# Linear attention with 32-row tiles and three level batches a chunk, LRU input projections between them, gate projections behind

## The chip, the cores and the metric

The kernel runs on one core of a Trainium2 chip. The metric is the device time of one execution in microseconds; lower is better. TensorE (PE) multiplies, with its weight loads (PEld) as records of their own; VectorE (DVE), ScalarE (ACT) and GpSimd (POOL) work elementwise; SyncE (SP) starts transfers.

## What is computed

Two layers of a hybrid decoder over 1024 tokens of width 1024, all in float32. Each layer normalises its input to h, projects it with one matrix, runs four mixers beside each other, gates and projects back:

```python
h = rms_norm(x, norm_g)
(gate, a_q, a_k, a_v, a_g, b_q, b_k, b_v, b_f, c_q, c_kv, c_kr, d_x) = jnp.split(h @ w_in, points, axis=-1)
ya = gla_mixer(a_q, a_k, a_v, a_g, ...)      # gated linear attention, 8 heads, 32 key and 64 value columns each
yb = fox_mixer(...)                          # softmax attention with a forget gate
yc = mla_mixer(...)                          # latent attention
yd = rglru_mixer(d_x, ...)                   # convolution of width 4, two gates, linear scan
y = jnp.concatenate([ya, yb, yc, yd], axis=-1) * jax.nn.silu(gate)
return x + y @ w_out
```

The linear attention (group A) is a scan over chunks of positions. Inside a chunk, with G the cumulated log decay of each key column:

```python
A = jnp.sum(q_[:, :, :, None, :] * k_[:, :, None, :, :] * decay, axis=-1)    # decay = exp(G_t - G_s), s <= t
o = einsum('bhtk,bhkv->bhtv', q_ * exp(G), S) + einsum('bhts,bhsv->bhtv', A, v_)
S_new = exp(G_last)[..., None] * S + einsum('bhsk,bhsv->bhkv', k_ * exp(G_last - G), v_)
```

and its output is normalised per head. Group D (the LRU) is `h = a * h_before + b` over positions, with a and b from two gates.

## The kernel before

**Projections.** h lies in SBUF as two tiles, `h_hi` (rounded) and `h_lo` (the rest), both 128 partitions (8 blocks of the contraction) by 1024 tokens. w_in comes in chunks of mostly 256 columns (1 MB each) into two sets of buffers used in turn. `load_chunk` (SP) waits until the last chunk of its set is split; `round_chunk` (ScalarE, L186) makes `w_hi`, when the last unit of the set's earlier chunk is done; `split_chunk` (GpSimd, L193) makes `w_lo`. `project` computes a unit of output in one PSUM bank with 24 matmuls, 8 for each of the products w_hi h_hi, w_hi h_lo, w_lo h_hi (L227). A chunk of kind "C" has 4 units of 512 columns, one of kind "T" 8 units of 256. Units take banks 0 to 3 in turn (`RING = 4`), and `wait_bank` makes TensorE wait until the unit four before has been taken out. The names: q, k and v1, v2 (group A), gA0, gA1 and gD0, gD1 (gates), dx0, dx1 (LRU input), fq1, fk1, fv1 (group B), outA, outD (parts of the output projection, L478, added to the rows by VectorE at L508).

**Order.** Each engine runs one in-order program, written out by hand (`tensor_gla`, `scalar_lru`, `vector_gla`, `gpsimd_program`, `sync_gla` and so on), with semaphores between them. TensorE does q, `turn_a`, k, `z`, gA0, gA1, then eight chunks of linear attention, gD0 and outA; then the LRU stage: dx0, gate products of channel block 0 (`gates_pe`, L981, 4 matmuls), two units of gD1, block 1, gD1, dx1, block 2, fq1 with block 3 in it, fk1, fv1, outD.

**Linear attention** (`Gla`). q and k are held transposed: two groups g of 128 partitions, each with 4 heads of 32 partitions. A chunk has 128 tokens. Its causal matrix A is split by 7 levels: at level j blocks of 64 >> (j-1) tokens are paired, and the scores of the later half against the earlier half are a product of decayed queries and keys with exponents taken relative to the edge between them, so that all are below zero. The diagonal comes from one undecayed product. So a chunk has 9 items (`NI`): 2 diagonal ones and 7 levels.
- `exponent` (VectorE, L702 and L703, 14 passes of 128x128) writes G relative to the edges to E; `decay` (ScalarE, L812 to L815) exponentiates it.
- `expand_q` (ScalarE, L805, 4 passes) writes q4, four copies of q, in which a head mask leaves one head each. Thus one matmul with 128 rows of contraction gives the scores of four heads side by side.
- `chunk_pool` (GpSimd) makes decayed keys `kl` (L680, 7 passes of 128x256) and the expanded decayed queries `ql` of levels 2, 4, 6; `expand` (L666, two passes a level) on VectorE makes the others. Both have three slots.
- `products_pe` (TensorE) computes an item into one of four banks: a diagonal item is one matmul of 512 columns (L853), a level two of 256 (L864).
- `mask` (VectorE) puts an item into A: the diagonal by a product with the identity (L715, 128x512), a level by a predicated copy (L724, 128x512).
- `finish` (TensorE), a chunk later and behind the first five items of the next: transposes of the end keys (L876), the output product (L882 with the state S, L885 with A, 8 matmuls of 64 columns), the state product (L892).
- Then `state` (VectorE, L756, 8 pieces of 32x64), squares, `means`, root, `normalise` (L768), and `turn_y` and `y_evac`, which transpose a chunk of output and multiply it by its gate.

A float32 matmul shows as two records of load and two of matmul, an fp32r one as one of each.

**Products with 64 output partitions.** In the softmax attentions `pv` (L1379) writes 64 output partitions, for the even head 0 to 63, for the odd one 64 to 127; two calls follow each other. L1318 and L367 are transposes, as L902.

**LRU** (`Lru`). For each of four blocks of 128 channels: `conv` (VectorE, L1007, L1009), `gates_pe`, `gates_act` (ScalarE sigmoids, L1022, L1025), `gx`, `decay_act` (Tanh L1037, Exp L1040, Square L1043), `u`, `root_act` (Sqrt L1055), `scan` (VectorE, L1061 to L1065). ScalarE loads a table (ACT_TABLE_LOAD) between kinds of functions. `zero_blocks` (GpSimd) and `load_blocks` (SP) prepare the gate weights. `sync_fox` loads outD's rows and weights when the last scan is done.

Of the kernel before, what the change touches and what calls it, by code (L numbers as in the profile page):

```python
# [24 lines left out]
HH = 4  # L25
# [18 lines left out]
RING = 4  # L44
# [40 lines left out]
class Trunk:  # L85


    def __init__(self, nc, dram, out, ctx):
# [23 lines left out]
        self.chunks, self.chunk_of, self.units, self.unit_of = [], {}, [], {}  # L112
        self.w_landed = [self.sem(f"w_landed{i}") for i in range(2)]
# [31 lines left out]
    def add_unit(self, layer, name, part, by):  # L145
        j = self.chunk_of.get((layer, name))
        if j is not None:
            self.chunks[j]["units"].append(len(self.units))
        nth = 1 + sum(1 for unit in self.units if unit[2] == by)
        self.unit_of[layer, name, part] = len(self.units)  # L150
        self.units.append((j, part, by, nth))
# [49 lines left out]
    def bank(self, u):  # L201
        return self.psum[:, u % RING, :]

    def wait_bank(self, pe, u):
        if u >= RING:
            _, _, by, nth = self.units[u - RING]
            pe.wait_ge(self.evac_sem[by], nth)

    def project(self, pe, layer, name, *part):
        u = self.u(layer, name, *part)  # L210
        j, part, _, _ = self.units[u]
# [3 lines left out]
        self.wait_bank(pe, u)  # L215
        if first:
            pe.wait_ge(self.w_rounded, j + 1)
        for n, (w, h) in enumerate(((w_hi, self.h_hi), (w_hi, self.h_lo), (w_lo, self.h_hi))):
            if n == 2 and first:
                pe.wait_ge(self.w_split, j + 1)  # L220
            for kk in range(KT):
                if c["kind"] == "C":
                    m, half = part
                    lhs, rhs, o = w[:, kk, m * P:(m + 1) * P], h[:, kk, half * BANK:(half + 1) * BANK], self.bank(u)
                else:
                    lhs, rhs, o = h[:, kk, part * P:(part + 1) * P], w[:, kk, :], self.bank(u)[:, :width]
                last = pe.matmul(o, lhs, rhs, start=(kk == 0 and n == 0), stop=(kk == KT - 1 and n == 2))  # L227
        last.then_inc(self.unit_done, 1)
# [10 lines left out]
    def evacuated(self, eng, layer, name, *part):  # L239

        _, _, by, nth = self.units[self.u(layer, name, *part)]
# [20 lines left out]
def plan_layer(k, layer):  # L262
# [24 lines left out]
    chunk("k", "C", C_AK, CHUNK, 1)  # L287
    gate("gA0", 0, 0, 0)
# [3 lines left out]
    chunk("dx0", "C", C_DX, CHUNK, 1)  # L292
    gate("gD1", 3, 1, 0)
    chunk("dx1", "C", C_DX + CHUNK, CHUNK, 1)
# [216 lines left out]
class Gla:  # L511


    NI = GN + LEVELS
    MIDDLE = GN + 3
    HALF = P // 2
    IN, END = LEVELS, LEVELS + 1
    NB, B_OUT, B_STATE, B_KT, B_Y = 4, 4, 5, 6, 7
    ON_POOL = (2, 4, 6)
    ON_DVE = (1, 3, 5, 7)  # L520
    R = 3
    N16 = SEQ // BANK

    def __init__(self, k, layer):
        self.k, self.layer = k, layer
        HALF, NI = self.HALF, self.NI
        self.qT = k.area("gla_qT", A_QT, [P, GN, SEQ])
        self.kT = k.area("gla_kT", A_KT, [P, GN, SEQ])
        self.v = k.area("gla_v", A_V, [P, TT, GROUP_W])
        self.G = k.area("gla_G", A_GATE0, [P, GN, SEQ])  # L530
        self.sg = k.area("gla_gate", A_SG, [P, CT, SEQ])
        self.E = k.area("gla_E", A_E, [P, 2, LEVELS + 2, GN, P])
        self.aT = k.area("gla_aT", A_E, [RANK, SEQ])
        self.e = k.area("gla_e", A_E + 4096, [P, GN, SEQ])
        self.k_et = k.area("gla_k_end_tok", 84032, [P, GN * P])
# [8 lines left out]
        self.rstd = k.area("gla_rstd", s + 1280, [P, HEADS])  # L544
        self.a_tok = k.area("gla_a", A_TOK, [P, TT, RANK])
        w = W_SET[1]
        self.S = k.at("gla_S", w, [P, GN, HH, HEAD])
        self.masks = k.at("gla_masks", w + 2048, [P, LEVELS, HALF], I32)
        self.q4 = k.at("gla_q4", w + 3840, [P, GN, HH, P])
        w += SET  # L550
        self.A = k.at("gla_A", w, [P, 2, HEADS, P])
        self.ql = k.at("gla_ql", w + 8192, [P, self.R, GN, HH, HALF])
        self.kl = k.at("gla_kl", w + 14336, [P, self.R, GN, P])
        n = {"gla_loaded": 80, "masks_loaded": 16, "a_turned": self.N16, "a_copied": self.N16, "z_done": GN * self.N16,
             "z_biased": GN * self.N16, "logs": 1, "exponents": TT, "decays": TT, "q_expanded": TT,
# [2232 lines left out]
```

## Time and profile before

| what | value |
|---|---|
| time, median of 3 runs | 2696.1 us (2695.87 to 2705.18) |
| profiled execution, from first to last instruction | 2699.1 us |
| TensorE busy | 2458.8 us, 91% |
| VectorE, ScalarE, GpSimd busy | 1280.1, 972.9, 862.0 us |
| share of TensorE in the chain that ended last | 79% |
| linear attention chunks, layer 1 | 172.4 to 355.3 us |
| linear attention chunks, layer 2 | 1510.5 to 1693.3 us |

The span is that of one profiled execution, and no other time of that execution is shown. Busy time counts a record from its start to its end; matmul records overlap, so a busy TensorE can still have room. The chain follows the last instruction back to what released it, step by step.

### The profile page before, as it was taken

The page shows a single profiled execution, that of the slowest core. Times are in us where ns is not written, and L with a number is a line of the kernel's source. Part 1 is how long each engine was busy: PE and PEld are TensorE (multiplying, and loading weights), DVE is VectorE, ACT ScalarE, POOL GpSimd, SP SyncE. Part 2 cuts the span into 40 slices and gives each one's busy share as a digit, 9 for nine tenths or more (in the row PEclk, how much of TensorE's full clock was granted, in tenths as well). Part 3 has the DMA queues.
Part 4 walks back from the last instruction along what each step waited for, and adds up shares of the span by engine and source line. Part 5 has one row for each costly group of instructions (what it writes and reads, how often), then busy time and mean ns, then how long its engine had stood idle before and what let it go on. Part 6 is the DMA issues. An engine that isn't in the chain of part 4 may idle for free.

```text
span 2699.1 us, 32797 instructions
## 1 busy us (share of the span) xinstructions
PE 2458.8 (91%) x13104; PEld 1870.4 (69%) x13104; DVE 1280.1 (47%) x1966; ACT 972.9 (36%) x1596; POOL 862.0 (32%) x726
## 2 busy tenths in 40 slices
PE   7977699998999999899999766999989999998998
PEld 7755477897577695655697555779865866856556
DVE  4049934543514325565431698236344153265653
ACT  4232214632433433344433222155324243333441
POOL 1225522211441620154411455121205225202542
PEclk9988899999999999999999888999999999999999
DMA  4100043041010021200321000422300101122003
GB/s 137 51 0 1 1 132 107 17 156 47 1 48 1 13 74 57 95 23 1 126 79 35 1 1 1 160 79 69 135 16 1 48 1 45 42 89 85 1 1 117
DMA packets 91864, 141.15 MB, mean 52 GB/s; under 512 B 18208, under 2 KB 65344, under 8 KB 91712
## 3 DMA queue, kind: packets, MB, share of 16 engines
q1 hardware_dynamic: 91712, 139.05, 15.1%
q8 instruction: 105, 1.72, 0.3%
q14 instruction: 47, 0.39, 0.0%
HBM read 105.48 MB, written 33.55 MB: 52 GB/s over the span
## 4 chain that ended last, share of the span: by engine, by line
PE 79%; DVE 15%; issue 3%; ACT 2%; POOL 1%; DMA 0%; POOLq 0%; SPq 0%; DVEq 0%; ACTq 0%
PE psum L227 36%; PE psum L478 12%; PE psum L1379 6%; PE psum L1364 4%; PE psum L1333 3%; PE psum L1365 3%; PE psum L1367 3%; PE psum L864 3%; PE psum L1346 2%; PE psum L1318 2%; DVE gla_E L703 2%; DVE gla_ql L666 2%; DVE gla_A L724 2%; PE psum L1386 1%; DVE gla_S L756 1%
## 5 line engine op out<-in xcount | busy, mean ns | idle before, releaser
L193 POOL TENSOR_TENSOR w_lo<-w_raw,w_hi 128x2048 fp32r<-128x2048 f32 (+3 forms) x60 | 278.2, 4638 | 970.5 <-ACT w_hi L186 970.5
L864 PE MATMUL psum<-gla_ql,gla_kl 128*128 128x256 f32 x448 | 147.5, 484 | 115.4 <-DVE gla_ql L666 111.7
L864 PEld LDWEIGHTS psum<-gla_ql,gla_kl 128*128 128x128 f32 x448 | 105.8, 248 | 162.1 <-DVE gla_A L724 112.4
L227 PE MATMUL psum<-h_hi,w_hi 128*128 128x512 f32 x768 | 199.3, 403 | 0.0
L1577 POOL TENSOR_TENSOR mla_acc<-mla_acc,mla_p 128x512 f32<-128x512 f32 (+3 forms) x160 | 160.2, 1015 | 107.9 <-ACT mla_p L1447 106.5
L227 PE MATMUL psum<-w_hi,h_hi 128*128 128x256 f32 (+3 forms) x1280 | 186.2, 289 | 4.7 <-ACT w_hi L186 4.7
L227 PE MATMUL psum<-h_lo,w_hi 128*128 128x512 f32 x768 | 190.1, 390 | 0.0
L227 PE MATMUL psum<-h_hi,w_lo 128*128 128x512 f32 x768 | 189.8, 390 | 0.0
L227 PE MATMUL psum<-w_hi,h_lo 128*128 128x256 f32 (+3 forms) x1280 | 182.2, 286 | 0.0
L227 PE MATMUL psum<-w_lo,h_hi 128*128 128x256 f32 (+3 forms) x1280 | 179.8, 283 | 1.8 <-POOL w_lo L193 1.8
L186 ACT ACTIVATE w_hi<-w_raw 128x2048 fp32r<-128x2048 f32 (+3 forms) x60 | 113.4, 1894 | 187.1 <-PE psum L478 174.3
L1577 POOL TENSOR_TENSOR fox_acc<-fox_acc,fox_p 128x512 f32<-128x512 f32 (+3 forms) x160 | 148.7, 946 | 89.6 <-ACT fox_p L1447 88.8
L227 PEld LDWEIGHTS psum<-w_hi,h_hi 128*128 128x128 f32 x1280 | 167.4, 194 | 10.9 <-issue 9.3
L508 DVE TENSOR_TENSOR x_rows<-x_rows,psum 128x512 f32<-128x512 f32 x128 | 85.7, 685 | 180.1 <-PE psum L478 152.1
L227 PEld LDWEIGHTS psum<-h_hi,w_hi 128*128 128x128 f32 x768 | 146.3, 193 | 34.5 <-issue 4.9
L227 PEld LDWEIGHTS psum<-w_hi,h_lo 128*128 128x128 f32 x1280 | 167.8, 195 | 0.0
L227 PEld LDWEIGHTS psum<-w_lo,h_hi 128*128 128x128 f32 x1280 | 164.9, 192 | 2.2 <-POOL w_lo L193 2.2
L227 PEld LDWEIGHTS psum<-h_lo,w_hi 128*128 128x128 f32 x768 | 144.7, 188 | 30.4
L227 PEld LDWEIGHTS psum<-h_hi,w_lo 128*128 128x128 f32 x768 | 144.2, 188 | 29.9
L680 POOL TENSOR_TENSOR gla_kl<-gla_kT,gla_E 128x256 f32<-128x256 f32 x112 | 90.4, 815 | 214.7 <-PE psum L864 113.8
L1447 ACT ACTIVATE fox_p<-psum 128x512 f32<-128x512 f32 (+1 forms) x192 | 94.0, 489 | 136.6 <-PE psum L1369 109.1
L1447 ACT ACTIVATE mla_p<-psum 128x512 f32<-128x512 f32 (+1 forms) x192 | 93.8, 489 | 132.8 <-PE psum L1369 106.3
(321 smaller groups left out, 4827.7 us busy)
## 6 DMA issues: line engine op xcount, KB each, us to landing
w_raw<-in_w_in_dram SPq DMA_DIRECT2D x38, 1024.0 KB, 5.2
out_dram<-x_rows SPq DMA_DIRECT2D x64, 512.0 KB, 2.7
x_rows<-out_dram SPq DMA_DIRECT2D x56, 512.0 KB, 5.6
w_raw<-in_w_out_dram SPq DMA_DIRECT2D x16, 1024.0 KB, 5.2
x_first<-in_x_dram SPq DMA_DIRECT2D x8, 512.0 KB, 7.4
x_rows<-in_x_dram SPq DMA_DIRECT2D x8, 512.0 KB, 6.6
w_raw<-in_w_in_dram SPq DMA_DIRECT2D x2, 1088.0 KB, 8.9
w_raw<-in_w_in_dram SPq DMA_DIRECT2D x2, 1056.0 KB, 5.1
```

What stands on the lines that cost most here:

```text
L186: act.activation(self.w_hi[c["set"]][:, :n], self.w_raw[c["set"]][:, :n], ACT.Copy).then_inc(self.w_rounded, 1)
L193: pool.tensor_tensor(self.w_lo[c["set"]][:, :n], self.w_raw[c["set"]][:, :n], self.w_hi[c["set"]][:, :n].bitcast(F32), ALU.subtract).then_ ...
L227: last = pe.matmul(o, lhs, rhs, start=(kk == 0 and n == 0), stop=(kk == KT - 1 and n == 2))
L478: last = pe.matmul(k.bank(u), y, w[:, c, :], start=(c == 0 and i == 0), stop=(c == CT - 1 and i == 2))
L508: dve.tensor_tensor(at, at, ps, ALU.add).then_inc(k.evac_sem["dve"], 1)
L680: pool.tensor_tensor(self.kl[:, m % self.R, :, :], self.kT[:, :, self.tok(c)], self.E[:, c % 2, j - 1, :, :], ALU.mult).then_inc(self.k_le ...
L864: last = pe.matmul(k.psum[:, n % self.NB, g * HH * self.HALF:(g + 1) * HH * self.HALF], self.kl[:, m % self.R, g, :], self.ql[:, m % self. ...
L1333: last = pe.matmul(out, q[:M_ROW, a, x * P:(x + 1) * P], kk[:M_ROW, a, :hi - lo], start=True, stop=not diagonal)
L1364: pe.matmul(out, self.k_hi[ks][:R, a, keys], self.q_hi[qs][:R, a, lo:], start=True, stop=False)
L1379: pe.matmul(self.k.psum[a * HEAD:(a + 1) * HEAD, 4 + i % 2, lo:], self.pairs[p]["v"](a, kb), self.p[:, u % self.PR, lo:], start=(kb == 0), ...
L1447: act.activation(self.p[:, u % self.PR, lo:], self.k.psum[:, u % 2, lo:], ACT.Exp).then_inc(self.exp_done.sem, 1)
L1577: pool.tensor_tensor(acc, acc, p, ALU.add).then_inc(self.acc_done.sem, 1)
```

## The change

**Score products.** The queries are no longer expanded. Each head's scores come from a matmul of its own with 32 rows of contraction, the head's 32 partitions (a row tile of TensorE), and go to the bank of the head's number in its group (banks 4 to 7). `level_products` multiplies, in E itself, only the earlier halves by the keys, and writes the later halves times the queries to `ql`, on GpSimd alone: two passes of 128x128 a level. A chunk has three batches: the diagonal with levels 1, 2; levels 3, 4, 5; levels 6, 7. Between batches TensorE runs one of the three products of a dx unit (`product`, a third of `project`), unit c of dx0 and dx1 in chunk c. `mask_batch` masks a batch, the diagonal in one pass of 1024 columns; A has one buffer. The state S is 128 x 2 x 64, its product is 8 matmuls of 32 output columns, and VectorE writes a copy `S_bd` with zeros between heads for the output product.

**Order.** `turn_a` and `z` go between the q units. gA0 and gA1 come behind the chunks; their units have the y transposes between them, now four token tiles of one channel block at a time (`GROUPS` = 8). The dx units use banks 2 and 3 alone (`k.ring`). ScalarE evacuates dx inside the chunks. The first two convolutions run ahead of outA's additions. In the LRU stage the gate products are: blocks 0 and 1 after two units of gD1, block 2 after 7 parts of fq1, block 3 after one part of fk1; ScalarE and VectorE treat blocks in pairs, and ScalarE takes out all fq1 parts ahead of the third block's sigmoids. Several tiles have other places in SBUF.

```diff
     def chunk_pool(self, pool, c):
...
+        for b, levels in enumerate(self.BATCHES):
+            if c >= 1:
+                pool.wait_ge(self.scored.sem, self.scored.at(self.NBATCH * (c - 1) + b + 1))
+            for level in levels:
+                last = self.level_products(pool, c, level)
+            last.then_inc(self.products.sem, 1)
...
+    def level_products(self, eng, c, level):
+        e = self.halves(self.E[:, c % 2, level - 1, :, :], level)
+        q, kk = (self.halves(x[:, :, self.tok(c)], level) for x in (self.qT, self.kT))
+        eng.tensor_tensor(e[:, :, :, 0, :], kk[:, :, :, 0, :], e[:, :, :, 0, :], ALU.mult)
+        ql = self.ql[:, level - 1, :, :].rearrange("p g (n b) -> p g n b", b=self.HALF >> (level - 1))
+        return eng.tensor_tensor(ql, q[:, :, :, 1, :], e[:, :, :, 1, :], ALU.mult)
...
+    def scores(self, pe, c, b):
+        n = self.NBATCH * c + b
...
+        else:
+            pe.wait_ge(self.masked.sem, self.masked.at(self.OPS * c + self.BATCHES[b][0]))
+        if b == 0:
+            out = self.scores_at(0, -2, P)
+            for g in range(GN):
+                for i in range(HH):
+                    r = slice(DK * i, DK * (i + 1))
+                    pe.matmul(out[:, i, g, :], self.kT[r, g, self.tok(c)], self.qT[r, g, self.tok(c)], start=True, stop=True)
+        pe.wait_ge(self.products.sem, self.products.at(n + 1))
+        for x, level in enumerate(self.BATCHES[b]):
+            out = self.scores_at(b, x, self.HALF)
+            for g in range(GN):
+                for i in range(HH):
+                    r = slice(DK * i, DK * (i + 1))
+                    last = pe.matmul(out[:, i, g, :], self.E[r, c % 2, level - 1, g, :], self.ql[r, level - 1, g, :],
+                                     start=True, stop=True)
+        last.then_inc(self.scored.sem, 1)
...
     def mix_dve(self, dve, link, c):
...
         if c + 1 < TT:
             self.exponent(dve, c + 1)
+        self.mask_batch(dve, c, 0)
         if c >= 1:
+            self.state(dve, link, c - 1)
             self.means(dve, link, c - 1)
+        self.mask_batch(dve, c, 1)
         if c >= 1:
             self.normalise(dve, c - 1)
+        self.mask_batch(dve, c, 2)
...
+    def mix_pe(self, pe, c, between):
+        self.scores(pe, c, 0)
+        if c >= 1:
+            self.finish(pe, c - 1)
+        between(pe, 0)
+        self.scores(pe, c, 1)
+        between(pe, 1)
+        self.scores(pe, c, 2)
+        between(pe, 2)
...
 def tensor_gla(pe, k, a):
...
     for c in range(TT):
-        a.gla.mix_pe(pe, c)
-    a.gla.finish(pe, TT - 1)
+        gla.mix_pe(pe, c, lambda pe, n: k.product(pe, L, f"dx{c // 4}", n, *C_PARTS[c % 4]))
+    k.project(pe, L, "gA0", *C_PARTS[0])
+    gla.finish(pe, TT - 1)
+    k.project(pe, L, "gA0", *C_PARTS[1])
+    pe.wait_ge(gla.normed.sem, gla.normed.at(TT))
+    for i, part in enumerate(C_PARTS[2:]):
+        k.project(pe, L, "gA0", *part)
+        gla.turn_y(pe, i)
+    for i, part in enumerate(C_PARTS):
+        k.project(pe, L, "gA1", *part)
+        gla.turn_y(pe, 2 + i)
...
 def scalar_lru(act, k, link, a):
...
+    for t in range(TT):
+        fox.evac(act, "fq", t)
     lru.gates_act(act, 2)
+    lru.gates_act(act, 3)
     lru.decay_act(act, link, 2)
+    lru.decay_act(act, link, 3)
     lru.root_act(act, 2)
...
     lru.root_act(act, 3)
```

## Rows read from the trace of the kernel before

**Rows 1.** the page's first line
```profile
span 2699.1 us, 32797 instructions
```

**Rows 2.** busy time by stretches: length, then busy us (records) of each engine, granted clock
```profile
172.40:355.30 182.90, 121.02 (x488) 90.19 (x488) 161.70 (x318) 47.79 (x97) 101.60 (x122) 0.82 0.00 1
1510.50:1693.30 182.80, 120.44 (x488) 89.32 (x488) 161.50 (x318) 47.55 (x97) 101.65 (x122) 0.82 0.00 1
...
422.70:571.00 148.30, 148.30 (x898) 129.42 (x897) 76.60 (x56) 88.64 (x113) 29.75 (x6) 1.00 0.21 70
```

**Rows 3.** the chain: start us, us, engine, line, records
```profile
99.00 21.79 PE psum L227 x96
...
510.41 60.63 PE psum L227 x504
...
1345.17 1.75 PE psum L367 x16
```

**Rows 4.** waits from 217 to 342 us: who waits for whom, us, times, longest
```profile
PE psum L864 <- DVE gla_ql L666: 40.6, 16, 5.3
PEld psum L864 <- DVE gla_A L724: 39.9, 11, 5.7
```

**Rows 5.** timeline, L853 and a `finish`: start us, us, engine, line, tiles, records
```profile
243.34 1.88 PE L853 MATMUL psum<-gla_q,gla_kT 128*128 128x512 f32 x4
...
248.92 0.30 PEld L882 LDWEIGHTS psum<-gla_S,gla_E 128*128 128x128 f32 x2
...
250.58 1.08 PEld L885 LDWEIGHTS psum<-gla_v,gla_A 128*128 128x128 f32 x8
...
251.57 0.73 PEld L892 LDWEIGHTS psum<-gla_v,gla_k_end_tok 128*128 128x128 f32 x4
```

**Rows 6.** timeline of TensorE, pairs of `pv`
```profile
698.35 0.44 PE L1379 MATMUL psum<-fox_p,fox_v 128*64 128x128 f32 x4
...
701.14 1.08 PE L1379 MATMUL psum<-fox_p,fox_v 128*64 128x512 f32 x4
```

**Rows 7.** loads of `pv`: ns min/median/max of one; then the timeline of one pair's
```profile
L1379 PEld LDWEIGHTS psum<-fox_p,fox_v x384: 132/135/138, 686.9 to 2269.8; 128*64 128x64 f32 x192
...
701.14 0.20 PEld L1379 LDWEIGHTS psum<-fox_p,fox_v 128*64 128x64 f32 x4 [0.36 <-issue]
```

**Rows 8.** tile gla_A: ns min/median/max of one
```profile
L724 DVE COPY_PREDICATED gla_A<-gla_masks,psum x112: 691/719/1329, 181.9 to 1689.3; 128x512 f32<-128x512 int32 x112
L715 DVE TENSOR_TENSOR gla_A<-psum,ident x32: 672/676/679, 179.4 to 1670.9; 128x512 f32<-128x512 f32 x32
```

**Rows 9.** tile gla_E: ns min/median/max of one
```profile
L703 DVE TENSOR_TENSOR gla_E<-gla_G x112: 275/281/4578, 152.3 to 1654.2; 128x128 f32<-128x128 f32 x112
...
L687 POOL TENSOR_TENSOR gla_E<-gla_qT,gla_E x16: 719/726/767, 188.6 to 1681.7; 128x256 f32<-128x256 f32 x16
```

**Rows 10.** timeline at the first chunk
```profile
175.53 1.68 ACT L812 ACTIVATE gla_E<-gla_E 128x1792 f32<-128x1792 f32 x1
...
178.25 1.86 POOL L680 TENSOR_TENSOR gla_kl<-gla_kT,gla_E 128x256 f32<-128x256 f32 x2 [50.44 <-ACT gla_E L815]
...
189.48 0.81 DVE L702 TENSOR_TENSOR gla_E<-gla_G 128x128 f32<-128x128 f32 x1
```

**Rows 11.** timeline of ScalarE in the LRU
```profile
502.95 0.69 ACT L1022 ACTIVATE lru_dx<-psum,lru_vec 128x512 f32<-128x512 f32 x1
...
508.45 1.28 ACT L1040 ACT_TABLE_LOAD   x1
509.75 1.15 ACT L1040 ACTIVATE lru_dx<-lru_dx,lru_small 128x1024 f32<-128x1024 f32 x1
```

**Rows 12.** timeline of VectorE in the LRU
```profile
496.53 8.16 DVE L1009 SCALAR_TENSOR_TENSOR lru_xc<-lru_dx,lru_conv_w,lru_xc 128x1024 f32<-128x1024 f32 x3
```

**Rows 13.** timeline ahead of outD
```profile
542.64 1.26 SPq L174 DMA_DIRECT2D w_raw<-in_w_out_dram  x2
...
552.51 1.92 ACT L186 ACTIVATE w_hi<-w_raw 128x2048 fp32r<-128x2048 f32 x1 [4.25 <-DMA w_raw<-in_w_out_dram]
```

More of the change, by code:

```diff
@@ L43 @@
 CHUNK_MAX = CHUNK + RANK
-RING = 4
 BASE = 16512
@@ L214, in project @@
         w_hi, w_lo = (w[c["set"]][:, :KT * width].rearrange("p (k n) -> p k n", n=width) for w in (self.w_hi, self.w_lo))
-        self.wait_bank(pe, u)
-        if first:
+        if n == 0:
+            self.wait_bank(pe, u)
+        if n == 0 and first:
             pe.wait_ge(self.w_rounded, j + 1)
[L218 to L228, printed above, removed]
+        if n == 2 and first:
+            pe.wait_ge(self.w_split, j + 1)
+        w, h = ((w_hi, self.h_hi), (w_hi, self.h_lo), (w_lo, self.h_hi))[n]
+        for kk in range(KT):
+            if c["kind"] == "C":
+                m, half = part
+                lhs, rhs, o = w[:, kk, m * P:(m + 1) * P], h[:, kk, half * BANK:(half + 1) * BANK], self.bank(u)
+            else:
+                lhs, rhs, o = h[:, kk, part * P:(part + 1) * P], w[:, kk, :], self.bank(u)[:, :width]
+            last = pe.matmul(o, lhs, rhs, start=(kk == 0 and n == 0), stop=(kk == KT - 1 and n == 2))
+        if n == 2:
+            last.then_inc(self.unit_done, 1)
     def wait_unit(self, eng, layer, name, *part):
@@ L291, in plan_layer @@
     out("outA", 0, 1)
-    chunk("dx0", "C", C_DX, CHUNK, 1)
-    gate("gD1", 3, 1, 0)
-    chunk("dx1", "C", C_DX + CHUNK, CHUNK, 1)
+    gate("gD1", 3, 1, 1)
     chunk("fq1", "T", C_BQ + HALF_W, HALF_W, 0)
@@ L568, in load @@
+         self.out_done, self.state_product, self.state_new, self.squares, self.mean, self.rstd_ready, self.normed,
+         self.y_turned, self.y_ready, self.end_decays) = (Signal(k, name, count) for name, count in n.items())
     def load(self, sp):
@@ L905, in mix_pe @@
[L905 to L908 removed]
+                for i in range(HH):
+                    r = slice(DK * i, DK * (i + 1))
+                    at = GN * P + g * HEAD
+                    last = pe.matmul(k.psum[r, self.B_END, at:at + HEAD], self.k_et[:, g * P + DK * i:g * P + DK * (i + 1)],
+                                     self.v[:, c, g * HALF_W + i * HEAD:g * HALF_W + (i + 1) * HEAD], start=True, stop=True)
@@ L2574, in gpsimd_program @@
             gla.chunk_pool(pool, c)
-            if c == 0:
-                k.split_chunk(pool, L, "gD0")
+            if c == 2:
+                k.split_chunk(pool, L, "dx1")
             if c == 6:
-                a.outA.rest(pool, 0)
-        for name in ("outA0", "outA1", "dx0"):
+                k.split_chunk(pool, L, "gA0")
+        for name in ("gA1", "gD0", "outA0"):
+            k.split_chunk(pool, L, name)
+        for name in ("outA1", "gD1", "fq1"):
             k.split_chunk(pool, L, name)
@@ L2583, in gpsimd_program @@
         a.lru.zero_blocks(pool)
-        for name in ("gD1", "dx1", "fq1", "fk1", "fv1", "outD0", "outD1", "gB1"):
+        for name in ("fk1", "fv1", "outD0", "outD1", "gB1"):
             k.split_chunk(pool, L, name)
@@ L2645, in sync_gla @@
     lru.load(sp)
-    for name in ("outA1", "dx0", "gD1"):
+    for name in ("gD0", "outA0", "outA1", "gD1", "fq1"):
         k.load_chunk(sp, L, name)
@@ L2649, in sync_gla @@
     lru.load_blocks(sp)
-    for name in ("dx1", "fq1", "fk1", "fv1"):
+    for name in ("fk1", "fv1"):
         k.load_chunk(sp, L, name)
```

530 lines of the change are left out of this document (226 added, 304 removed).

## The prediction

> **What bounds the kernel now.** I read the page first: one core, a span of 2699.1 us [rows 1], TensorE busy for 91% of it, and the chain of waits runs over TensorE for 79% of the span. A stage is therefore worth what TensorE idles or wastes in it. The busy time by stretches shows where that is: in the linear attention of either layer (182.9 and 182.8 us) TensorE is busy 121.0 and 120.4 us at a mean granted clock of 0.82, while VectorE is busy for some 162; the projection and LRU stretch behind it runs at 148.3 busy us of 148.3, clock 1.00 [rows 2]. The chain gives the price of a projection: 96 matmuls of 512 columns in 21.79 us, 0.227 each, so a unit of 24 costs 5.45 us; units of 256 columns cost 504 x 0.120, 2.9 us for 24 [rows 3]. The wait table of six chunks names the loop: level matmuls wait for VectorE's expansion (L666) and their loads for its masks (L724) [rows 4]. These are six chunks in 125 us, 20.8 each.
>
> So the linear attention is a ping-pong of VectorE and TensorE with TensorE half empty, and the change can win by filling it. It moves both dx chunks, 8 units, 43.6 us a layer, into the eight row chunks. The stage and these units cost 182.9 + 43.6 = 226.5 us a layer before. All other projections keep their price wherever they stand.
>
> **The decisive unknown: the small matmuls.** Per row chunk the change makes 64 matmuls with 32 rows of contraction (8 of 128 columns, 56 of 64) in place of 2 of 512 and 14 of 256. No row tile is in this trace. The nearest rows are of two kinds. Full-height matmuls of 64 columns (L885): 8 records in 1.08 us, two records to a matmul, 0.27 us each [rows 5]; 64 of them would be 17.3 us a chunk. And column tiles: `pv` (L1379) sends pairs to output partitions 0 to 63 and 64 to 127. A pair takes 1.08 us at 512 columns and 0.44 at 128 [rows 6], where two full-height float32 matmuls of 512 columns (L853) take 1.88 [rows 5]: the pair costs little more than one. Its four loads lie within 0.20 us although each takes 0.135 [rows 7]. So two tiles compute and load at the same time. Four row tiles, each with its own bank (head i of a group goes to bank 4+i), are the same pattern turned. I take four matmuls in the time of one, 0.27 us a round: 16 rounds, 4.3 us a chunk. The bounds are 4.3 below and 17.3 above. I stand near the first, since L1379 is a tile row and L885 is not.
> The Trainium skill ("TensorE: Matmul & The Clock Gate", part 3 on packing small matmuls) states a 3.07-fold gain for four row tiles; by it the 17.3 us would be an estimated 5.6 us and the time some 21 us later than mine; the trace shows the column kind only.
> Each change of tile shape may wait until the array is empty. A pair of 128 columns takes 0.44 us, of which the slope between 128 and 512 columns, 0.64 / 3, explains 0.21 [rows 6]; the other 0.23 is filling and emptying. 8 changes a chunk, 16 chunks: between nothing and 29 us in all. I take 9, nearer to nothing, since filling and emptying lie partly beside the neighbours' and half of the changes fall where TensorE has spare time. "TensorEngine Tiling (Array Packing)" of the Trainium skill (Key Properties) says that a mode switch drains; no row here shows it.
>
> **One chunk, step by step** (us from the start of `scores` batch 0). Batches of 24, 24 and 16 small matmuls cost 1.5, 1.5 and 1.0, and 0.2 until another engine sees them.
> - TensorE: batch 0 until 1.5; `finish` of the chunk before: transposes 0.4, then output product 2.65 (248.92 to 251.57 [rows 5]), seen at 4.7. State product until 5.2 (it was 4 records, now 8 matmuls with 32 output columns; between 0.3 and 1.0, taken 0.6). Then a third of a dx unit, 1.8, until 7.0.
> - VectorE: batch 0 mask from 4.8: one 1024-wide pass 1.3 (two of L715's 0.68) and two of L724 at 0.72 to 0.75 [rows 8], until 7.6. TensorE's batch 1 waits for that: 7.7 to 9.2; dx until 11.0.
> - VectorE: state 1.1 (one pass of 512 columns at 0.68, two small ones) and means 0.95 (the same and a small one) until 9.6; mask batch 1, three times 0.75, until 11.8; normalise 0.7 until 12.5. TensorE's batch 2: 11.9 to 12.9, dx until 14.7. Mask batch 2: 13.1 to 14.5.
> - The next batch 0 starts at 14.7. `exponent`, 14 passes of 0.28 (L703 [rows 9]), runs from 14.5 to 18.4, under the next batch 0 and `finish` (19.5).
> Thus the period is 14.7, with TensorE busy some 13.5 of it. ScalarE (decay 2.8, copies, square, dx evacuation, root: under 6) and GpSimd (14 products of half the width of L687's 0.73 [rows 9], taken 0.45, and two whole: 7.8) are below it. The expansion on VectorE, ScalarE's four q4 copies and the 32-partition state pieces are removed: they are already missing in this sum.
> What queues behind new waits: TensorE's in-order stream puts dx products behind each mask wait, so a late mask delays both. Batch b of `chunk_pool` waits for the same batch a chunk earlier; `decay` ends near 6, so its products have 7 us to spare.
>
> **Beginning and end.** Projections of the output gates used to cover the decay sums and the first exponentials; the k units (21.8 us) cover the sums now, z being moved ahead of them. Not covered: evacuation of the last k part 0.8, table load 1.28 [rows 11], the E passes and a small copy (175.53 to 178.25), together 4.9, and four products 1.8: 7.0 us with scale factors [rows 10]. Chunk 0 has no `finish`: 1.7 + 2.8 + 1.7 + 2.3 + 1.2 + 1.5 = 11.2. Seven more are 102.9. The last `finish` is 3.0, and seven of the eight rounds of y transposes, inside the stage before, now stand beside projections: 4.2. A layer: 7.0 + 11.2 + 102.9 + 3.0 + 4.2 = 128.3 against 226.5, so 98.2 less.
>
> **What is given back.** A split on GpSimd holds a VectorE pass: the longest of L703 took 4.58 us, the length of a split, and ordinary GpSimd products stretch 0.28 to 0.81 [rows 9, 10]. Two splits (dx1, gA0) now fall inside the chunks, as gD0's and outA's did; I charge 4 us a layer.
> The LRU loses the dx units that covered it. With D the end of outA, TensorE runs 2 gD1 units, 4+4 gate products (8 x 0.86), 2 units, 7 fq units: the third gate set is due at D+49, the last fq unit ends at D+55. ScalarE takes all 8 fq parts first and then sigmoids (0.69 each), Tanh, Exp, Square and Sqrt of two channels (1.15 a pass, 1.28 a table load [rows 11]): until D+64 with TensorE's fourth gate set, decays 4.7 and 6.0, roots 3.5, fv1 rounding 1.95: D+80.5. Only then is fk part 0 evacuated. With four banks, fk part 4 waits from D+73 to D+81: 8 us. The block weights' DMA, now behind the fq1 split, comes about 2 us late, the third convolution (up to 8.2 us under a split [rows 12]) 1.5, the bank waits 0.5: 12 us a layer. The scans (about 4.7 each with their two products) end near D+87; outD0's weights take 9.9 us from issue to rounding [rows 13], split near D+108, before TensorE needs them at D+117. Nothing to pay there; 14 us before. DMAs are otherwise moved into idle queues; SP's gD0 load now stands behind `out_done`, 27 us ahead of its use.
>
> **Sum.** 2699.1 - 2 x (98.2 - 4 - 12) + 9 = 2543.7 us of span. The median of the runs shown is 3.0 below that span, so 2541 us. Half a per cent, 13.5 us, is what I count as a difference.
>
> **Rivals.**
> - *Slower chain.* Tiles as taken, but GpSimd's products stretch the masks' neighbours and the period is 17.5 (exponents at L703's 0.81 end after the out product). For it: that row; against it: the exponents have 1.1 us of slack and the masks (L724, median 0.719) seldom stretch. 14 x 2.8 = 39 more: 2580. Chance 0.08.
> - *Half rate.* The two halves of an fp32 matmul go in order, so only two tiles overlap, all that rows 6 show: 8.6 us a chunk, period 19. A layer 15.8 + 133 + 14.2 = 163: 2610. Chance 0.13.
> - *Loads one at a time.* Matmuls overlap, loads of 128 columns don't: two loads of 0.109 (the fastest pace of load and matmul, 16 in 1.75 us in L367 [rows 3]) for each of 64, 14.0 us, period 23.5, 198.7 a layer: 2681. Rows 7 speak against it. Chance 0.12. The same page of the Trainium skill (LDWEIGHTS) says that a 32-row load costs as much as a 128-row load, which is this rival when loads do not overlap.
> - *No overlap, slower than before.* L885's 0.27 for each of the 64: period 27.5, a layer 24 + 192.5 + 14.2 = 230.7, 4 more than before, and the 16 given back stay: 2746. It decides from 0.22 us a small matmul (8 periods of 24). Chance 0.10.
>
> **How the numbers follow.** The forecast has 0.57: 2541, by itself 2500 (no LRU stall, no drains, no split stalls) to 2590. The range goes from 2495 over the slower chain and the half rate to 2670, just short of serial loads. Faster: 0.57 + 0.08 + 0.13 and half of the fourth: 0.84; same 0.07; slower 0.09.
>
> **What would show it.** In the profile after: 24 small matmuls in about 1.5 us (6.5 would be no overlap); dx matmuls between L864's successors; a period near 14.7; clock 1.00 in the chunks; a 7 us gap ahead of the first; a TensorE wait for fk's evacuation of about 8 us. The forecast is wrong if the small matmuls take over 0.1 us each or VectorE's period passes 15.

## The result and the profile after

The changed kernel takes 2560.4 us (median of 4 runs, 2558.3 to 2564.9) beside 2697.3 for the kernel before; the ratio is 0.949 with a 95% interval of 0.947 to 0.950. The forecast was 2541 us with a range of 2495 to 2670. The profiled execution has a span of 2563.1 us, against the 2543.7 that the prediction's sum gives: 19.4 us more. The median is 19.4 us above the forecast too.

Busy time by stretches of the kernel after (start:end, length, then busy us and records of TensorE's matmuls, its loads, VectorE, ScalarE and GpSimd, the granted clock, DMA share, GB/s):

```profile
126.50:261.20 134.70, 112.95 (x1483) 91.86 (x1483) 106.06 (x201) 38.34 (x72) 70.93 (x130) 0.94 0.03 9
196.58:212.00 15.42, 13.71 (x190) 11.18 (x190) 13.14 (x29) 4.47 (x9) 7.66 (x17) 1.00 0.00 1
160.41:181.18 20.77, 16.61 (x190) 13.50 (x191) 17.45 (x29) 4.47 (x9) 12.64 (x18) 0.84 0.17 52
380.00:500.00 120.00, 110.04 (x712) 97.14 (x711) 59.03 (x45) 70.23 (x95) 19.97 (x6) 0.97 0.20 70
```

The first line answers to the first of [rows 2]: the stage of eight row chunks takes 134.7 us with the eight dx units (43.6 us) inside it, where it took 182.9 without them, and its clock is 0.94 in place of 0.82. The second line is an ordinary chunk, the third the chunk behind the split of dx1. The fourth is the LRU part, which had no idle TensorE time before and has 10 us now.

The ordinary chunk on TensorE (timeline: start us, us, engine, line, tiles, records; two records to a matmul; in brackets the idle time ahead and what ended it):

```profile
196.58 0.73 PE L722 MATMUL psum<-gla_qT,gla_kT 32*128 32x128 f32 x16 [0.77 <-DVE gla_A L750]
197.13 1.02 PE L729 MATMUL psum<-gla_ql,gla_E 32*128 32x64 f32 x32
198.08 0.44 PE L856 MATMUL psum<-ident,gla_E 128*128 128x128 f32 x2
...
204.05 1.57 PE L729 MATMUL psum<-gla_ql,gla_E 32*128 32x64 f32 x48 [0.54 <-DVE gla_A L750]
205.55 2.12 PE L237 MATMUL psum<-h_lo,w_hi 128*128 128x512 f32 x8
208.05 1.12 PE L729 MATMUL psum<-gla_ql,gla_E 32*128 32x64 f32 x32 [0.38 <-DVE gla_A L750]
```

Batch 0 runs from 196.58 to 198.08, 1.5 us; batch 1, 24 small matmuls, takes 1.57; batch 2, 16 of them, 1.12. These are the 1.5, 1.5 and 1.0 of the prediction: 0.065 us a matmul, a quarter of what L885 pays for 64 columns at full height [rows 5]. The weight loads of a batch 1 (here the one of the chunk before) overlap as well: 48 records of 0.18 to 0.19 us each lie within 1.43 us, so the rival of loads one at a time is out:

```profile
188.63 1.43 PEld L729 LDWEIGHTS psum<-gla_ql,gla_E 32*128 32x128 f32 x48 [0.93 <-DVE gla_A L750]
```

VectorE in the same chunk:

```profile
201.22 1.23 DVE L742 TENSOR_TENSOR gla_A<-psum,ident 128x1024 f32<-128x1024 f32 x1 [1.38 <-PE psum L866]
202.48 1.52 DVE L750 COPY_PREDICATED gla_A<-gla_masks,psum 128x512 f32<-128x512 int32 x2
...
205.78 2.21 DVE L750 COPY_PREDICATED gla_A<-gla_masks,psum 128x512 f32<-128x512 int32 x3
207.90 0.68 DVE L779 TENSOR_TENSOR gla_v<-psum,gla_rstd 128x512 f32<-128x512 f32 x1
209.24 2.71 DVE L750 COPY_PREDICATED gla_A<-gla_masks,psum 128x512 f32<-128x512 int32 x2 [0.65 <-PE psum L729]
```

Against the step-by-step chunk of the prediction, in us from its start: mask batch 0 begins at 4.64 (4.8 said), batch 1 at 9.20 (9.6), batch 2 at 12.66 (13.1). Up to here the chunk is a little ahead. But the last two masks take 2.71 us, not 1.4, and the next chunk starts at 15.42, not 14.7. GpSimd is no part of that: in the last chunk of the layer, where it has no products left, the same two masks take 2.66 us. They are levels 6 and 7, with blocks of two elements and of one; in type and number of elements they are like the other levels, so block size is the likely cause, though no run changes it by itself. The kernel before had it too, as this line of its timeline shows:

```profile
241.87 2.72 DVE L724 COPY_PREDICATED gla_A<-gla_masks,psum 128x512 f32<-128x512 int32 x2 [0.41 <-PE psum L864]
```

The maximum of 1329 ns in [rows 8] was these levels, two in every seven, and not a rare stretch.

The chunk behind the split of dx1, on GpSimd, VectorE and TensorE:

```profile
161.05 4.56 POOL L196 TENSOR_TENSOR w_lo<-w_raw,w_hi 128x2048 fp32r<-128x2048 f32 x1
...
161.16 4.60 DVE L697 TENSOR_TENSOR gla_E<-gla_G 128x128 f32<-128x128 f32 x1
...
170.70 2.84 PE L729 MATMUL psum<-gla_ql,gla_E 32*128 32x64 f32 x48 [3.36 <-DVE gla_A L750]
173.46 3.78 PE L237 MATMUL psum<-h_lo,w_hi 128*128 128x512 f32 x8
```

An exponent of 0.28 us is held for 4.60, as long as the split lasts. TensorE then idles for 3.36 us, and behind that idle stretch its records are nearly twice as long: 24 small matmuls take 2.84 us for 1.57, eight of 512 columns 3.78 for 2.1. That is the lower of its two clock levels (1.2 GHz in place of 2.4): the granted clock is 0.50 from 170.7 to 177.0 us. The stall costs 5.4 us (20.77 less 15.42), the other one in a layer 3.9.

The LRU part: TensorE, then ScalarE, then TensorE's waits from 380 to 500 us (who waits for whom, us, times, longest):

```profile
458.62 2.08 PE L237 MATMUL psum<-w_hi,h_hi 128*128 128x256 f32 x8 [5.51 <-ACT fox_k L1153]
460.50 1.91 PE L237 MATMUL psum<-w_hi,h_lo 128*128 128x256 f32 x8
...
471.75 1.21 PE L237 MATMUL psum<-w_hi,h_hi 128*128 128x256 f32 x8 [1.87 <-ACT fox_k L1153]
```

```profile
456.35 1.95 ACT L189 ACTIVATE w_hi<-w_raw 128x2112 fp32r<-128x2112 f32 x1
458.20 0.91 ACT L1153 ACTIVATE fox_k<-psum 128x256 f32<-128x256 f32 x3
...
481.33 1.91 ACT L189 ACTIVATE w_hi<-w_raw 128x2048 fp32r<-128x2048 f32 x1 [4.85 <-DMA w_raw<-in_w_out_dram]
```

```profile
PE psum L237 <- ACT fox_k L1153: 7.4, 2, 5.5
PE psum L981 <- issue: 1.2, 1, 1.2
PE psum L981 <- DVE lru_xc L1009: 1.1, 1, 1.1
```

fk's first evacuation comes directly behind the rounding of fv1's weights, as predicted, and TensorE waits 5.5 us for it. The other 1.9 us of the 7.4 are a second wait: the next fk evacuation stands behind the rounding of the scans' results, for which ScalarE waits. Behind the longer wait the clock is low again: a unit takes 5.3 us (458.62 to 463.91) for 2.9.

### The profile page after: what moved, and what is told of

It is laid out like the page before. It is cut to its first block, busy times and chain, and to the rows that moved or that the text cites. A ratio compares the mean times of both kernels' runs of the same rounds, so it can differ in the third digit from the quotient of the medians.

```text
span 2563.1 us, 35660 instructions
## 1 busy us (share of the span) xinstructions
PE 2378.3 (93%) x14804; PEld 1818.5 (71%) x14804; DVE 1163.1 (45%) x1756; ACT 917.1 (36%) x1508; POOL 792.6 (31%) x740
## 3 DMA queue, kind: packets, MB, share of 16 engines
q1 hardware_dynamic: 91712, 139.05, 15.8%
## 4 chain that ended last, share of the span: by engine, by line
PE 77%; DVE 15%; ACT 3%; issue 2%; POOL 1%; DMA 1%; SPq 0%; POOLq 0%; DVEq 0%; ACTq 0%
PE psum L237 32%; PE psum L491 12%; PE psum L1379 6%; PE psum L1364 4%; PE psum L1333 4%; DVE gla_A L750 3%; PE psum L1365 3%; PE psum L1367 3%; PE psum L1346 2%; PE psum L1318 2%; PE psum L729 2%; PE psum L1386 1%; PE psum L981 1%; PE psum L1766 1%; DVE mla_nm L1514 1%
## 5 line engine op out<-in xcount | busy, mean ns | idle before, releaser
L237 PE MATMUL psum<-h_hi,w_hi 128*128 128x512 f32 x768 | 204.5, 410 | 0.0
L237 PE MATMUL psum<-h_lo,w_hi 128*128 128x512 f32 x768 | 198.8, 402 | 0.0
L750 DVE COPY_PREDICATED gla_A<-gla_masks,psum 128x512 f32<-128x512 int32 x112 | 100.9, 900 | 26.2 <-PE psum L729 23.3
L1514 DVE TENSOR_REDUCE fox_nm<-psum 128x1 f32<-128x512 f32 (+3 forms) x128 | 71.8, 587 | 66.3 <-PE psum L1333 45.7
L1333 PE MATMUL psum<-mla_k_hi,mla_q_hi 96*128 96x512 f32 (+1 forms) x192 | 76.6, 434 | 26.5 <-DVE mla_nm L1514 15.2
```

Of the source, the lines that this page charges most:

```text
L750: dve.copy_predicated(self.halves(self.A[:, :, :], level)[:, :, :, 1, :], m, ps).then_inc(self.masked.sem, 1)
L1333: last = pe.matmul(out, q[:M_ROW, a, x * P:(x + 1) * P], kk[:M_ROW, a, :hi - lo], start=True, stop=not diagonal)
L1514: dve.tensor_reduce(out, self.k.psum[:, 2 + u % 2, :hi - lo], AX_X, ALU.max, negate=True).then_inc(self.max_done.sem, 1)
```

## Experiments

Each kernel is the changed one with the edit shown. The ratios are to the kernel before the change, measured beside them on the same chip.

**Does the low price come from overlapping row tiles?** Two runs change nothing but the order of the small matmuls. In the first, head by head (the loops of the diagonal are swapped in the same way):

```diff
...
-        for x, level in enumerate(self.BATCHES[b]):
-            out = self.scores_at(b, x, self.HALF)
-            for g in range(GN):
-                for i in range(HH):
+        for i in range(HH):
+            for x, level in enumerate(self.BATCHES[b]):
+                out = self.scores_at(b, x, self.HALF)
+                for g in range(GN):
```

> The score products of a batch are put in the order head by head, so that 4 to 6 consecutive small matmuls stand in the same 32 rows and the same bank; nothing else changes. Theory A (the low price, about 0.065 us a matmul in the trace, is overlap of four row tiles): a small matmul then costs 0.2 to 0.27 us, a batch of 24 some 5 to 6.5 us in place of 1.6, 9 to 13 us more a chunk, all of it on the ping-pong of TensorE and VectorE; 16 chunks: about 2560 + 180 = 2740 us (2700 to 2770), which is slower than the kernel before the change. Theory B (matmuls of 64 columns cost 0.065 us in any order, the rows do not matter): unchanged, 2560 us.

In the second, by pairs of heads:

```diff
...
-        for x, level in enumerate(self.BATCHES[b]):
-            out = self.scores_at(b, x, self.HALF)
-            for g in range(GN):
-                for i in range(HH):
...
+        for pair in ((0, 1), (2, 3)):
+            for x, level in enumerate(self.BATCHES[b]):
+                out = self.scores_at(b, x, self.HALF)
+                for g in range(GN):
+                    for i in pair:
...
```

> The score products go by pairs of heads (0 and 1 alternating, then 2 and 3), so that only two row tiles can work at once. Theory A: half the rate, about 0.13 us a matmul, a batch of 24 some 3.2 us; 4 us more a chunk: 2560 + 16 x 4 = 2625 us. This is the half-rate rival's price. Theory B: 2560 us. A third (two tiles already hide all that four do, since the two halves of an fp32 matmul go in order): 2560 to 2575.

The first took 2714.7 us (ratio 1.007, 1.003 to 1.011), the second 2603.3 us (0.963, 0.962 to 0.965). One batch of 24 at the full clock in the first run, and then in the second:

```profile
216.21 4.39 PE L729 MATMUL psum<-gla_ql,gla_E 32*128 32x64 f32 x48 [0.54 <-DVE gla_A L750]
```

```profile
213.98 2.51 PE L731 MATMUL psum<-gla_ql,gla_E 32*128 32x64 f32 x48 [0.52 <-DVE gla_A L752]
```

With 1.57 us for four row tiles, a small matmul costs 0.183 us with one tile at work, 0.105 with two and 0.065 with four. Theory A holds: the price is overlap, and the order of these loops is worth 154 us; in the wrong order the whole change is lost. Some 98 of the 154 are the batches themselves (6.1 us more a chunk at the full clock). The rest goes, as far as the traces tell, with the clock: the granted clock of the first run is 0.78 from 126.5 to 321.0 us, where the changed kernel has 0.94 in its chunks. Since head i always writes bank 4+i, matmuls that share a row tile here share a PSUM bank too; the two runs don't separate tile from bank. One tile is cheaper than my 0.2 to 0.27 and two tiles than 0.13, so both came out below the times expected (2740 and 2625). The half-rate rival is dead: four tiles do more than two. Its 2610 us was a fair price for two tiles all the same.

**What is filling worth?** The dx units leave the chunks:

```diff
-        gla.mix_pe(pe, c, lambda pe, n: k.product(pe, L, f"dx{c // 4}", n, *C_PARTS[c % 4]))
-    k.project(pe, L, "gA0", *C_PARTS[0])
+        gla.mix_pe(pe, c, lambda pe, n: None)
+    k.project(pe, L, "dx0", *C_PARTS[0])
     gla.finish(pe, TT - 1)
+    for part in C_PARTS[1:]:
+        k.project(pe, L, "dx0", *part)
+    for part in C_PARTS:
+        k.project(pe, L, "dx1", *part)
+    k.project(pe, L, "gA0", *C_PARTS[0])
```

ScalarE's evacuations and the rounding and split of gA0 move behind the chunks with them.

> The 8 dx units stand in one piece behind the chunks and not in thirds between the score batches. Theory A (the period of 15.4 us is a chain of masks on VectorE and score batches on TensorE, the thirds lie beside it and are free): the period stays at 15 to 16.5 (more where the granted clock falls), the units cost their 43.6 us a layer: 2560 + 87 + 0 to 16 = 2650 to 2665. Theory B (TensorE's stream bounds the period, 5.45 us of it are the thirds): the period falls by up to 5 us, the move costs nothing: 2560 to 2580. In either case what is left below 2697 is what cheaper scores gave without any filling.

It took 2704.2 us (ratio 1.002, 1.001 to 1.003): 144 us more than the change, and no faster than the kernel before. One chunk of it by busy time, and one batch of its timeline:

```profile
187.20:208.54 21.34, 13.87 (x166) 12.66 (x166) 13.20 (x30) 3.86 (x8) 7.66 (x18) 0.50 0.00 1
```

```profile
198.65 2.83 PE L729 MATMUL psum<-gla_ql,gla_E 32*128 32x64 f32 x48 [2.32 <-DVE gla_A L750]
```

Theory B is out. Theory A had the mechanism right (the thirds lie beside the chain) and the price too low: it allowed 0 to 16 us for the clock. TensorE, with shorter work and longer waits, is granted 0.50 of its clock throughout, a batch of 24 takes 2.83 us for 1.57, and the period is 21.3 us in place of 15.4. The six periods between the second chunk's start and the last's take 127.6 us (144.73 to 272.35) against 101.8 in the changed kernel, its two stalls included. So the units between the batches give twice: their own 43.6 us a layer, and the clock at which the scores run. Cheaper scores without filling gave nothing.

**The waits of the LRU part.** ScalarE evacuates fk early:

```diff
     lru.decay_act(act, link, 2)
+    fox.evac(act, "fk", 0)
     lru.decay_act(act, link, 3)
+    fox.evac(act, "fk", 1)
+    fox.evac(act, "fk", 2)
     lru.root_act(act, 2)
     lru.root_act(act, 3)
+    fox.evac(act, "fk", 3)
...
-    for t in range(3):
+    for t in range(4, 7):
         half.evac(act, "fk", t)
     act.wait_ge(a.lru.done.sem, a.lru.done.at(CT))
...
```

> ScalarE evacuates fk parts 0 to 3 between the decays and behind the roots of the second LRU pair, and parts 4 to 6 ahead of the wait for the scans. Theory A (TensorE's waits of 5.5 and 1.9 us at fk, and the stretch at the low clock behind the first, come from ScalarE's order alone): 7.4 of waits and 3 of low clock go in each layer, some 10 x 2: 2560 - 20 = 2540 us. Theory B (the LRU stage is bound by the scans and what outD needs, so the wait moves on to outD0's weights or to lru_y): 0 to -5 us, and a new wait of TensorE of 8 us at outD or fv.

2566.6 us (2563.3 to 2574.1): nothing won. The waits at fk are gone, and one of 12.2 us stands at fv. TensorE, ScalarE and SyncE of that run:

```profile
487.47 2.13 PE L237 MATMUL psum<-w_hi,h_hi 128*128 128x264 f32 x8 [12.19 <-ACT fox_v L1150]
```

```profile
482.09 1.91 ACT L189 ACTIVATE w_hi<-w_raw 128x2048 fp32r<-128x2048 f32 x1 [6.76 <-DMA w_raw<-in_w_out_dram]
```

```profile
469.34 0.34 SPq L1082 DMA_DIRECT2D fox_b<-in_fox_b_f_dram  x1
...
473.74 1.04 SPq L177 DMA_DIRECT2D w_raw<-in_w_out_dram  x2
```

SyncE waits for the scans (469.3), issues seven small and row transfers, and only then outD0's weights; ScalarE waits for these with fv's evacuations behind it. So next, fv parts 0 to 2 ahead of that rounding:

```diff
-    k.round_chunk(act, L, "outD0")
-    half.root_act(act, link, 0)
-    half.evac(act, "fv", 0)
-    half.evac(act, "fv", 1)
+    for t in range(3):
+        half.evac(act, "fv", t)
+    k.round_chunk(act, L, "outD0")
+    half.evac(act, "fv", 3)
+    half.root_act(act, link, 0)
     half.square_act(act, 1)
```

> As the run with fk evacuated between, and ScalarE also evacuates fv parts 0 to 2 ahead of the rounding of outD0's weights, for which it waits until 482 us in that run. Theory A (the wait is one of ScalarE's in-order queue and moved from fk to fv because fv stood behind that rounding): both waits and the low clock behind them go, 10 us a layer: 2540 us (2535 to 2547). Theory B (the chain scans, rounding of the results, outD weights sets when outD can start, whatever the queue): outD starts at 498 as before, 2560.

2557.7 us (2556.7 to 2560.3), 3 less. outD starts at 490.6, 8 us earlier, but TensorE waits just ahead of its first matmul and again inside the first group:

```profile
490.60 2.80 PE L491 MATMUL psum<-w_hi,lru_y_hi 128*128 128x512 f32 x8 [2.13 <-ACT fox_v L1150]
496.31 3.78 PE L491 MATMUL psum<-w_hi,lru_y_hi 128*128 128x512 f32 x8 [2.91 <-ACT fox_v L1150]
```

The wait had moved a third time, to the last fv parts. In time theory B was nearer (2560), though not in its sign, since outD did start earlier: ScalarE's queue was late by its wait for the weights, whatever stood behind. The remedy is the load itself:

```diff
+    k.load_chunk(sp, L, "outD0")
     sp.wait_ge(a.lru.done.sem, a.lru.done.at(CT))
...
-    for name in ("outD0", "outD1", "gB1", "gB0"):
+    for name in ("outD1", "gB1", "gB0"):
```

Alone, and with both edits of ScalarE's order:

> Only the load of outD0's weights moves ahead of SyncE's wait for the scans; ScalarE's order stays. Theory A (both are needed: the load hides ScalarE's wait of 5 to 7 us, and the order of fk and fv turns the time won into TensorE's): TensorE's waits at fk (7.4 us a layer) stay, since they end before that load is waited for; outD starts as before: 2560 us (2555 to 2562). Theory B (the late load alone sets the end of the LRU part): 2545 us.

> The early load with fk and fv evacuated between, without the edits to splits and convolution. Theory A: both TensorE's waits at fk and the low clock behind them go and nothing takes their place but some 2 us at outD: 8 us a layer, 2560 - 16 = 2544 us. Rival (the gain of the combined version came from the second convolution and the splits): 2556.

Alone 2564.8 us (2558.8 to 2565.6), nothing; its stretch from outA's first product to outD's takes 166.5 us for 165.4. Together 2546.7 us (2544.9 to 2549.1), 14 less than the changed kernel (7 a layer; 8 expected). TensorE's waits from 380 to 500 us in the latter:

```profile
PE psum L491 <- ACT fox_v L1150: 2.2, 1, 2.2
PE psum L981 <- issue: 1.2, 1, 1.2
PE psum L981 <- DVE lru_xc L1009: 1.1, 1, 1.1
PE psum L237 <- ACT fox_v L1150: 0.4, 1, 0.4
```

With the load alone, TensorE still waits at fk:

```profile
PE psum L237 <- ACT fox_k L1153: 8.4, 2, 5.5
```

So ScalarE's order and the early load are each worth 0 to 3 us alone: with the new order alone the last fv parts come too late, with the load alone the waits at fk stay. Both together are worth 14.

**The splits.** Once on GpSimd at another place, ahead of its products for batch 1:

```diff
                 pool.wait_ge(self.scored.sem, self.scored.at(self.NBATCH * (c - 1) + b + 1))
+            if b == 1 and split:
+                self.k.split_chunk(pool, self.layer, split)
...
-            if c == 2:
-                k.split_chunk(pool, L, "dx1")
-            if c == 6:
-                k.split_chunk(pool, L, "gA0")
+            gla.chunk_pool(pool, c, {3: "dx1", 7: "gA0"}.get(c))
```

> The splits of dx1 and gA0 stay on GpSimd but run behind the level batch 1 of a chunk, where VectorE's passes (masks, normalise) read PSUM, and not behind a chunk's products, where VectorE's exponents read SBUF alone. Theory A (a GpSimd pass of 4.6 us holds a VectorE pass only when that reads and writes SBUF alone; masks run on): each of the two stalls of 3.75 us goes, but GpSimd's later products now meet the exponents and take back 1 to 2: -2 to -4 us a layer, 2560 - 6 = 2554. Theory B (any VectorE pass is held): the stall falls on the masks, which are on the chain: 2560 to 2568.

And once on VectorE (and no longer in GpSimd's program):

```diff
     for c in range(TT):
+        if c == 3:
+            gla.k.split_chunk(dve, gla.layer, "dx1")
+        if c == 7:
+            gla.k.split_chunk(dve, gla.layer, "gA0")
         gla.mix_dve(dve, link, c)
```

> The splits of dx1 and gA0 run on VectorE itself, ahead of the exponents of chunk 4 and of chunk 7's masks; one such pass is 2.1 to 2.3 us there. Theory: a stall of 3.75 us is replaced by a pass of 2.2: for dx1's, 1.5 us less and some of it hidden in the 1.4 us that VectorE waits in each period; for gA0's the same: 3 to 6 us a layer less, 2560 - 9 = 2551. Rival: it is not the held pass that makes these two chunks 5 and 4 us longer but the weights' arrival; then 2560 or more.

2548.6 us (ratio 0.945, 0.944 to 0.947) and 2546.1 us (0.944, 0.942 to 0.945): 12 and 14 less than the changed kernel, more than either theory gave. The first of them, GpSimd and then VectorE:

```profile
169.02 4.59 POOL L196 TENSOR_TENSOR w_lo<-w_raw,w_hi 128x2048 fp32r<-128x2048 f32 x1 [1.47 <-PE psum L731]
```

```profile
169.08 2.24 DVE L752 COPY_PREDICATED gla_A<-gla_masks,psum 128x512 f32<-128x512 int32 x3
171.22 0.68 DVE L781 TENSOR_TENSOR gla_v<-psum,gla_rstd 128x512 f32<-128x512 f32 x1
172.56 2.68 DVE L752 COPY_PREDICATED gla_A<-gla_masks,psum 128x512 f32<-128x512 int32 x2 [0.66 <-PE psum L731]
```

Theory A holds: beside a split of 4.59 us the masks and the normalise, which read PSUM, take 2.24, 0.68 and 2.68 us as ever, where an exponent was held for 4.60. The Trainium skill says it the same way ("SBUF — State Buffer", Who interferes with whom: a VectorE instruction with at most one SBUF input, outside the two-port modes, does not contend with GpSimd; with two, the later one waits until the first has finished), and the rows agree.

From the second chunk's start to the last's it is 94.6 us in the first run and 93.3 in the second, for 101.8: of the 9.3 us that the two stalls of a layer cost, 7.3 and 8.5 are won. In the first run one chunk takes 17.4 us, where GpSimd's late products stand beside exponents of 0.5 to 0.8 us each. My sizes were off because I counted the held pass and not the low clock behind it; for the first run my own figures (two stalls of 3.75 less 1 to 2) also give more than the 2 to 4 us a layer that I wrote. That the weights' arrival makes the two chunks long is out, since both runs shorten them.

**Together.** First the two edits of ScalarE's order and the splits on VectorE; then also the early load, and the scales and second convolution behind outA's first additions; then the same with the splits beside the masks.

```diff
+    a.outA.add(dve, *OUT_GROUPS[0])
     lru.scales_dve(dve, link)
     lru.conv(dve, link, 1)
-    for h, n in OUT_GROUPS:
+    for h, n in OUT_GROUPS[1:]:
         a.outA.add(dve, h, n)
```

> Both edits: fk and fv evacuated between, and the two splits on VectorE. If the two losses are separate, their gains add: 20 of the LRU part and the 14 that the splits on VectorE gave: 2526 us. If the first theory on fk and fv is wrong, 2546.

> The version before with two more edits: outD0's weights are loaded ahead of the wait for the scans (ScalarE's 7 us wait for their DMA goes), and the scales and the second convolution stand behind the first group of outA's additions (TensorE's wait of 2.05 us a layer for them goes). 4 us less than the version before for the convolution (2 x 2.05), and 0 to 2 for the load, which is hidden then: 2521 us. If the second convolution then comes late for the gate products or the adds fall behind, it stays at 2526.

> The version before, with the splits on GpSimd beside the masks in place of VectorE. The two ways of splitting differed by 2.5 us in their medians, inside their spread: 2521 to 2525 us; a lead of more than 4 us for either would say that what GpSimd's later products take from the exponents (0.5 to 0.8 us each in that run) is not hidden.

2547.6 us (2544.5 to 2551.6), 2527.2 us (2524.5 to 2528.7; ratio 0.936, 0.934 to 0.937) and 2529.6 us (2526.3 to 2532.0). The first missed its 2526: without the early load the order is worth little, as above. The second and third missed 2521 and 2521 to 2525, which were counted from that 2526; from the first they fell by 20 and 18 us where 4 to 6 were expected, since the load that I priced at 0 to 2 us is what makes the order count (14 us in the runs above). The second is the fastest kernel here, 33 us below the changed one. Its parts add up: 14 (LRU part), 14 (splits), 4 (convolution, two waits of 2.05 us, not measured by itself) make 32. The two ways of splitting don't differ by what these runs can tell.

## Why the prediction was right, and where it was off

The 19.4 us between the sum and the profiled span are found by the starts of the same groups in both traces. The first product of outA starts at 377.7 before and 333.0 after in layer 0, that of outD at 570.9 and 498.4; in layer 1 they are 1715.7 and 1601.6, 1908.8 and 1768.0, and the first product of the layer is at 1359.6 and 1287.7.

- *Small matmuls at 0.27 us a round of four, 4.3 us a chunk*: right. Measured 1.50 + 1.57 + 1.12 = 4.2. The Trainium skill's 3.07-fold gain for four row tiles ("TensorE: Matmul & The Clock Gate", part 3) was weighed against L885's 0.27 us, which was the wrong base: one tile alone costs 0.183 us here, and four gain 2.8-fold on it in a batch of 24. The break-even of 0.22 us a matmul was too high as well: at 0.183 the first experiment is already at 1.007, since the clock was not in that estimate.
- *Changes of tile shape, 9 us in all*: not seen as a term. Batches of 16 and 24 differ by 0.45 us, 0.056 a matmul; what is left of a batch is 0.2 us, and its neighbours' records overlap it. No run separates it.
- *Period 14.7*: 15.42, above the 15 that the prediction named as a sign of being wrong; the sign was set too tight, since 0.7 us in 14 periods are 10 us. Mis-sized in one term, the last mask batch: 2.7 us for 1.4, by the median of [rows 8]. The terms before it were 0.5 us too long. The rival of a slower chain named 17.5 and GpSimd's products as the cause (its 0.81 us is a row of L702, not L703); what lengthened the chain was the masks of the two smallest blocks.
- *Beginning 7.0 and chunk 0 11.2*: 5.4 (126.5 to 131.95) and 13.0 (to 144.93). The table load that I charged was not there; the first batch ran at the low clock behind the gap.
- *Split stalls, 4 us a layer*: 9.3 (5.4 and 3.9), mis-sized: the low clock behind each stall was left out.
- *Stage as a whole*: 89.7 us less a layer (98.2 less the splits' 4 and half of the 9), measured 88.3 (377.7 - 333.0 + 43.6) and 85.8 (356.1 - 313.9 + 43.6, from the first product of layer 1). That it came so near is in part luck. Beginning and chunks took 134.7 us (126.5 to 261.2) where 7.0 + 11.2 + 102.9 and 4 for the splits were summed, 9.6 more. This was made good by the 4.5 a layer for changes of tile shape, which no run shows, and by 2.3 us that I hadn't counted: the stage starts 45.9 us earlier (172.4 to 126.5) where the gate units account for 43.6. The rest lies in the last `finish` and the transposes, and I haven't separated it.
- *LRU part gives back 12 us a layer*: 15.8 (193.2 - 165.4 = 27.8, taken from 43.6) and 16.9. The fk wait foreseen as 8 was 5.5; a second one of 1.9, not foreseen, brings the sum to 7.4, so that the near hit is luck. Block weights 1.2 (2), convolution 1.1 (1.5), bank waits 0.2 (0.5). Not foreseen either were 2.4 of low clock behind the fk wait and 2.05 at outA, where VectorE's second convolution holds the additions. These make 14.4 of the 15.8; the other 1.4 are not assigned. "Nothing to pay" at outD was right only because TensorE was late already: with fk mended, the load named in [rows 13] was next.
- *The rest*: of the 19.4 us the stages are 5.3, the LRU parts 8.7; the remaining 5.4 lie in stretches that the change doesn't touch, 4.8 of them behind outD of layer 1. There this execution took 752.4 us (from the start of outD's last group to the end), the kernel before 747.6. The experiments, which leave that stretch as it is, took 747.0 to 752.6: spread of executions, and no cost of the change that could be told from it.

So the mechanism held, and so did the direction and size of both sides of the sum, in size with the luck named above. What was off were durations that a median or a single row hid, and the same omission three times (chunk 0, splits, fk): what TensorE's clock does behind a wait.

## What to carry to other kernels

Small matmuls on row tiles are worth their packing only if consecutive ones stand in different tiles, and if TensorE has other work to fill the waits of the chain: here either alone gave nothing. Price a stall of TensorE with the slow records behind it, and read minimum and maximum of a group beside its median before a duration enters a chain. When an engine's queue is late, move what it waits for (here a load behind another engine's wait) and the work queued behind it together; one alone only moves the wait on.

## What the runs showed of the hardware

- Float32 matmuls with 32 rows and 64 columns, each head's tile with a bank of its own, cost 0.183, 0.105 and 0.065 us with one, two and four row tiles in turn. Eight of 128 columns take 0.73 us in the four-tile order, 0.74 in the pair order and 0.75 head by head, where only two in a row share a tile: for such short runs the order made no difference.
- Behind a wait of 3.36 us TensorE was granted 0.50 of its clock for the next 6.3 us. Where it waited 2.3 to 2.8 us ahead of each batch, in the run with the dx units behind the chunks, it was 0.50 over six chunks; with waits of 0.4 to 0.8 us in the ordinary chunk it was 1.00.
- `copy_predicated` of 128 x 512 takes about 0.73 us at the levels with blocks of four elements and more, and about 1.35 at those with blocks of two and one.
- A GpSimd pass holds a VectorE pass that reads two operands from SBUF for its whole length (0.28 us became 4.60); passes with an operand in PSUM run beside it unchanged.
